# Hybrid decoder trunk on one core: masked copies of the gated heads in two halves a slot apart, the last pair's loads in another order, the fifth block's scores as 384 and 256 columns

## The reference

```python
h = rms_norm(x, norm_g);  proj = h @ w_in                 # split into the groups
# A: 12 heads of 64: dilated windows (128,1), (512,4), (2048,16), mixed by log-sum-exp
# B: 8 heads of 64: causal softmax with bias c[t] - c[s], c = cumsum(log sigmoid(f))
logits = q @ k.T + c[t] - c[s];  p = softmax(causal(logits));  out_b = p @ v
# C: 4 gated linear attention heads, key width 96, value width 192
S_t = diag(alpha_t) S_{t-1} + k_t^T v_t;  out_c = rms_norm(q_t S_t)
mixed = concat([out_a * silu(az), out_b * silu(bz), out_c * silu(cz)])
return x + mixed @ w_out
```

## Time and profile before

| | |
|---|---|
| median of 3 runs | 2104.77 us (2103.35 to 2106.62) |
| profiled execution | 2104.9 us, its span 2103.2 us |
| PE busy | 2050.0 us, 97% |
| DVE busy | 970.3 us, 46% |
| ACT busy | 858.4 us, 41% |
| POOL busy | 249.5 us, 12% |

### The profile page before, as it was taken

How to read it: one execution, slowest core, us unless ns; L and a number is a source line. 1 busy time by engine, 2 the same in 40 slices (tenths; PEclk the granted TensorE clock), 3 DMA queues, 4 the chain that set the end, 5 groups by cost and what they waited for, 6 DMA issues and landing times.

```text
span 2103.2 us, 28249 instructions
## 1 busy us (share of the span) xinstructions
PE 2050.0 (97%) x10120; PEld 1717.1 (82%) x10120; DVE 970.3 (46%) x1579; ACT 858.4 (41%) x1434; POOL 249.5 (12%) x181
## 2 busy tenths in 40 slices
PE   6999999999999999999999999999999988999999
PEld 5778888888878888888888888888888867788887
DVE  6611356455544544554454544554544465512122
ACT  6311344434444444454544444454544454311110
POOL 0000344252420101010010101010010100000000
PEclk9999999999999999999999999999999999999999
DMA  6322323433232222222222222223222363324134
GB/s 224 78 75 65 108 76 104 108 89 108 69 101 76 71 88 58 86 74 89 61 70 85 75 86 86 81 81 100 60 90 85 129 210 113 125 89 130 47 128 150
DMA packets 192457, 201.09 MB, mean 96 GB/s; under 512 B 15993, under 2 KB 141993, under 8 KB 191233
## 3 DMA queue, kind: packets, MB, share of 16 engines
q1 hardware_dynamic: 175664, 169.70, 27.2%
q10 hardware_dynamic: 16720, 30.45, 3.9%
HBM read 151.33 MB, written 48.78 MB: 95 GB/s over the span
## 4 chain that ended last, share of the span: by engine, by line
PE 84%; DVE 7%; ACT 4%; issue 3%; DMA 2%; POOL 1%; SPq 0%; DVEq 0%; ACTq 0%; POOLq 0%
PE acc L1851 18%; PE acc L1853 18%; PE acc L1852 18%; PE pv L2064 4%; PE turned L2049 4%; PE scores L2041 2%; PE scores L2038 2%; DVE w_lo L1360 1%; PE scores L2154 1%; PE scores L2155 1%; PE turned L2155 1%; PE acc L2155 1%; PE scores L2156 1%; PE turned L2156 1%; PE acc L2156 1%
## 5 line engine op out<-in xcount | busy, mean ns | idle before, releaser
L1851 PE MATMUL acc<-act_hi,w_hi 128*128 128x512 f32 x1856 | 743.0, 400 | 7.5 <-DVE act_lo L1391 2.4
L1853 PE MATMUL acc<-act_hi,w_lo 128*128 128x512 f32 x1856 | 725.8, 391 | 0.0
L1852 PE MATMUL acc<-act_lo,w_hi 128*128 128x512 f32 x1856 | 724.2, 390 | 0.0
L1851 PEld LDWEIGHTS acc<-act_hi,w_hi 128*128 128x128 f32 x1856 | 349.4, 188 | 77.1 <-DVE w_lo L1360 5.0
L1853 PEld LDWEIGHTS acc<-act_hi,w_lo 128*128 128x128 f32 x1856 | 348.6, 188 | 76.1
L1852 PEld LDWEIGHTS acc<-act_lo,w_hi 128*128 128x128 f32 x1856 | 349.7, 188 | 65.1
L1360 DVE TENSOR_TENSOR w_lo<-w_raw,w_hi 128x512 fp32r<-128x512 f32 x223 | 196.2, 880 | 317.4 <-ACT w_hi L934 317.4
L1677 DVE TENSOR_TENSOR pt_lo<-turned,pt_hi 128x1024 fp32r<-128x1024 f32 (+1 forms) x120 | 114.9, 958 | 256.0 <-ACT pt_hi L1234 255.0
L1226 ACT ACTIVATE prob<-prob,neg_max 128x128 f32<-128x128 f32 (+7 forms) x160 | 124.1, 776 | 251.5 <-DVE neg_max L1661 251.5
L1234 ACT ACTIVATE pt_hi<-turned 128x1024 fp32r<-128x1024 f32 (+1 forms) x120 | 97.6, 813 | 244.7 <-PE turned L2049 244.7
L934 ACT ACTIVATE w_hi<-w_raw 128x512 fp32r<-128x512 f32 x223 | 139.0, 623 | 128.8 <-PE acc L1853 105.4
(11 more groups left out here) (308 smaller groups left out, 2723.2 us busy)
## 6 DMA issues: line engine op xcount, KB each, us to landing
w_raw<-in_w_in_dram SPq DMA_DIRECT2D x240, 256.0 KB, 2.8
proj_scratch<-stage ACTq DMA_DIRECT2D x116, 256.0 KB, 2.1
w_raw<-in_w_out_dram SPq DMA_DIRECT2D x71, 256.0 KB, 3.0
raw<-proj_scratch SPq DMA_DIRECT2D x20, 512.0 KB, 3.2
act_lo<-mixed_scratch SPq DMA_DIRECT2D x7, 1024.0 KB, 6.7
res<-in_x_dram SPq DMA_DIRECT2D x24, 256.0 KB, 5.5
out_dram<-res SPq DMA_DIRECT2D x24, 256.0 KB, 2.8
extra_raw<-in_w_out_dram SPq DMA_DIRECT2D x23, 256.0 KB, 3.2
```

Source lines behind the costliest of these rows:

```text
L1851: pe.matmul(acc, hi, xh, start=first, stop=False)
L1852: pe.matmul(acc, hi, xl, start=False, stop=False)
L1853: mm = pe.matmul(acc, lo, xh, start=False, stop=end)
```

## The change

Three edits, and nothing else on any engine:

1. `put_first` is cut in two halves. The two copies from `scores` stay in slot 8, the two from `turned` go to slot 9, behind the differences of level 3 and ahead of the copy of level 1.
2. In the last pair SP issues three loads of mixed blocks one by one between rows 4, 5 and 6 instead of all three ahead of row 4; the load of the gate stands behind row 8 instead of row 6, the tiles of x behind row 10 instead of row 7, and the stores of partial sums (with the next tiles of x) behind rows 20 and 35 instead of 18 and 33.
3. Block 4's scores begin at column 128, so that they are 384 and 256 columns.

```diff
 def score_offset(j):
     i = j % NT
-    return HALF * (i % 2) if i < 4 else 0
+    return HALF * (i % 2) if i < 4 else P * (i == 4)
...
-            load_mixed(4)
-            load_mixed(5)
-            load_mixed(6)
             for n in range(4, EARLY):
+                if n < 7:
+                    load_mixed(n)
                 load_early_rows(n)
-                if n == 6:
+                if n == 8:
                     sp.wait_ge(mix_lo, KK_GATED + 1)
                     load_gate(LAST, last_column)
-                if n == 7:
+                if n == 10:
                     sp.wait_ge(silu_done, LAST)
                     for t in range(4):
                         load_early_residual(t)
                 for r, tiles in enumerate(ROUNDS[:-1]):
-                    if n == (KT - 1) * (r + 1) + 3:
+                    if n == (KT - 1) * (r + 1) + 5:
...
-                if slot == G_LEVEL[0] + 2:
-                    put_first(c)
+                for half in range(2):
+                    if slot == G_LEVEL[0] + 2 + half:
+                        put_first(c, half)
...
-            def put_first(c):
-                dve.wait_ge(gla_zero, c + 1)
-                dve.wait_ge(gla_lv, LEVELS * c + 1)
-                for half in range(2):
-                    to = ...
-                    if half > 0:
-                        dve.wait_ge(gla_put, levels_put)
-                    put(to, ident_both..., pieces[half][:, :, :, 0:P])
+            def put_first(c, half):
+                if half == 0:
+                    dve.wait_ge(gla_zero, c + 1)
+                    dve.wait_ge(gla_lv, LEVELS * c + 1)
+                to = ...
+                if half > 0:
                     dve.wait_ge(gla_put, levels_put)
-                    put(to..., level_mask[:, 0, :, :]..., pieces[half][:, :, :, P:])
+                put(to, ident_both..., pieces[half][:, :, :, 0:P])
+                dve.wait_ge(gla_put, levels_put)
+                put(to..., level_mask[:, 0, :, :]..., pieces[half][:, :, :, P:])
...
-                pe.wait_ge(masked, ITEMS * pair + j - (o > 0))
+                pe.wait_ge(masked, ITEMS * pair + j - (o == HALF))
                 q = q_st[:, h, i * P:(i + 1) * P]
-                for c0 in range(0, n, HALF):
-                    c1 = min(c0 + HALF, n)
+                edge = min(HALF - o % HALF, n)
+                for c0, c1 in ((0, edge), (edge, n))[:1 + (edge < n)]:
```

More of the change, by code:

```diff
@@ L1568, in put @@
                 dve.copy_predicated(dst, mask.bitcast(I32), data).then_inc(gla_put, 1)
-            def put_first(c):
-                dve.wait_ge(gla_zero, c + 1)
-                dve.wait_ge(gla_lv, LEVELS * c + 1)
-                for half in range(2):
-                    to = weights_t[:, half * HALF:(half + 1) * HALF].rearrange("p (b u q) -> p b u q", b=2, u=2)
-                    if half > 0:
-                        dve.wait_ge(gla_put, levels_put)
-                    put(to, ident_both[:, :, :].unsqueeze(1).broadcast_to([P, 2, 2, P]), pieces[half][:, :, :, 0:P])
+            def put_first(c, half):
+                if half == 0:
+                    dve.wait_ge(gla_zero, c + 1)
+                    dve.wait_ge(gla_lv, LEVELS * c + 1)
+                to = weights_t[:, half * HALF:(half + 1) * HALF].rearrange("p (b u q) -> p b u q", b=2, u=2)
+                if half > 0:
                     dve.wait_ge(gla_put, levels_put)
-                    put(to.rearrange("p b u (n two) -> p b u n two", two=2)[:, :, :, :, 1],
-                        level_mask[:, 0, :, :].unsqueeze(1).broadcast_to([P, 2, 2, HEAD]),
-                        pieces[half][:, :, :, P:])
+                put(to, ident_both[:, :, :].unsqueeze(1).broadcast_to([P, 2, 2, P]), pieces[half][:, :, :, 0:P])
+                dve.wait_ge(gla_put, levels_put)
+                put(to.rearrange("p b u (n two) -> p b u n two", two=2)[:, :, :, :, 1],
+                    level_mask[:, 0, :, :].unsqueeze(1).broadcast_to([P, 2, 2, HEAD]), pieces[half][:, :, :, P:])
             def put_level(c, l):
```

## The result

| | before | changed |
|---|---|---|
| median | 2104.56 us (2101.37 to 2106.62, 6 runs) | 2116.53 us (2112.18 to 2118.62, 6 runs) |
| profiled execution, its span | 2104.9, 2103.2 | 2112.18, 2110.4 |
| PE's mean granted clock, profiled | 0.993 | 0.991 |

The profiled execution of the changed kernel is the fastest of its six; the others took 2116.0 to 2118.6.

What follows compares the result with a forecast made beforehand. PE, busy almost throughout, was taken as the bound, so only its work or idle time counts. Terms of -1.8, -6.7 and +3.2 sum to -5.3 from 2104.77: 2099.5 us, stated range 2093.5 to 2105.5.

Steps and rivals of the forecast that it cites:

- Edit 3: Block 4's scores: 0.09 us less PE time in each of 20 items, -1.8 us, bounds -1.0 and -2.0.
- Edit 2: Last pair: quarter 7 starts 3.6 us earlier and quarter 11 6.7 earlier; -6.7 us, bounds -6.2 and -9.2.
- Rival B: Last pair: the next wait takes the gain, quarter 11 hardly earlier; -1 instead of -6.7, 2105.2 us; chance 0.15.
- Edit 1, levels 3 and 4: Gated heads: the level 3 wait goes, PE waits about 1.5 us at level 4, which starts 0.8 later.
- Rival A: Gated heads: differences come 1.7 us earlier and both waits go; -0.65 a head, -2.6, 2093.7 us; chance 0.20.
- Level 5 is 0.3 us in time again, level 6 more. So each head loses 0.8: Gated heads after level 4: no further delay at later levels, so +3.2 us in four heads.
- Rival C: Gated heads: the new 1.5 us wait at level 4 drops the clock, 1.7 to 2.5 us more where it falls; chance 0.15.

Runs made afterwards that it cites:

- last_pair_gate_row6: The kernel before with only the last pair's load order changed, but the gate's load kept behind row 6: 2101.51 us, ratio 0.999.
- halves_back_early: The kernel before with the two `turned` copies a slot later and ACT's reversed copy of the values two slots earlier: 2108.47 us, ratio 1.0022.
- halves_only: The kernel before with only the two copies from `turned` moved a slot later: 2125.12 us, ratio 1.0097.

## Why the prediction was wrong

Two of its three terms came out as forecast; the third, edit 1, had the right delay and missed one of its consequences.

**Edit 3: right in the records.** -1.8 was said, -1.9 is there for ten pairs; the medians cannot confirm it.

**Edit 2: right.** Quarter 7 lost its wait, quarter 11 came 6.7 earlier and still waits 3.27 (3.4 was said), and the edit alone gives 6.7 to 7.0 at the median. DVE's score step of block 6 began at 1736.52, 1722.69 without the offset of 13.83, where 1722.66 was said. Its cause was given a little too narrowly: last_pair_gate_row6 keeps some 2 us without moving the gate's load. Rival B falls.

**Edit 1, levels 3 and 4: right.** Second head, with the offset of 3.89: the second difference of level 4 was to end at 356.5 + 3.89 = 360.4, and the exponential behind it began at 360.42; `q_tile` was to end at 361.3 + 3.89 = 365.2, and PE's level 4 began at 365.24. The wait is 1.5, and level 4 is 365.24 - 360.62 - 3.89 = 0.73 later. Rival A falls: the second difference of level 3 ended at 353.65 + 1.76 - 3.89 = 351.52, which is 0.27 earlier than before and not 1.7. DVE, second head, a difference of level 1, the first copy from `scores`, both differences of level 3, a copy from `turned`; then POOL's instruction beside the first of these copies:

```profile
345.76 0.68 DVE L1518 TENSOR_TENSOR g_t<-g_b 96x512 f32<-96x512 f32 x1
...
350.31 0.75 DVE L1568 COPY_PREDICATED logit_bias<-ident_both,scores 128x512 f32<-128x512 int32 x1 [2.07 <-PE turned L1931]
...
352.51 1.21 DVE L1518 TENSOR_TENSOR g_t<-g_b 96x512 f32<-96x512 f32 x1
353.65 1.76 DVE L1519 TENSOR_TENSOR g_t<-g_b 96x512 f32<-96x512 f32 x1
355.33 0.73 DVE L1568 COPY_PREDICATED logit_bias<-ident_both,turned 128x512 f32<-128x512 int32 x1
...
349.81 1.54 POOL L882 TENSOR_TENSOR q_tile<-g_qd,g_t 96x512 f32<-96x512 f32 x1
```

The differences of level 3 take 1.21 and 1.76 beside POOL's work, where that of level 1, without POOL beside it, took 0.68. The copy with its data in PSUM takes 0.75 beside POOL's `q_tile`, and 0.73 at 355.33, where POOL is idle. The Trainium skill ("SBUF — State Buffer", section "Who interferes with whom") has the rule that a DVE instruction with two SBUF inputs contends with GpSimd's reads and one with a single SBUF input does not. The trace agrees.

**The step that failed** is "Level 5 is 0.3 us in time again, level 6 more. So each head loses 0.8". It followed POOL's `q_tile`, the one releaser that the earlier trace rows name, and passed over what stands between levels 4 and 5 on PE: the transposes of the values, whose releaser is ACT. Level 5 itself was in time, as said: its `q_tile` ended at 368.71 + 1.27 = 369.98, and PE came to it at 371.97, or at 370.5 without the new wait. But the exponential of level 5 was late with DVE's differences, and the values' copy behind it had 0.24 us in hand. This wait of 1.4 brings the loss from 0.8 to 2.4 a head, 9.5 us in four instead of 3.2. halves_back_early shows that: with the copy elsewhere the loss is 0.8 a head and 4.8 us in all.

**The clock** took the rest, 6 us in the profiled execution of the changed kernel and 4 x 3.3 = 13 in that of halves_only. The prediction gave it nothing in the gated heads, and named a granted clock below 1.00 there as a sign that it was wrong. Rival C had the mechanism but not its condition. It asked whether a wait of 1.5 is long enough, and held 0.15 for it; a wait of 1.5 alone kept 1.00 in three heads, and one of 1.25 alone in four. Waits of 1.5 and 1.4 (1.9 and 1.3 in the first head) with 369.62 - 1.44 - 367.04 = 1.1 us of work between them dropped the clock in all heads of halves_only, and in three of four in the changed kernel. C's highest time, 2109.5, was too low as well, since it had the waits at 0.8 a head. What made the second head of the changed kernel the exception is open.

## What to carry to other kernels

When a step on one engine comes later, list everything that stands behind it in that engine's program, and every engine that waits for any of it, not only the releaser that the view of waits names: a wait that is hidden by 0.24 us has no row there. An instruction that depends on nothing late should not stand behind one that does; here the place of such a copy of 1.04 us decided over some 17 us. And cost waits by their neighbourhood: two waits that were each harmless to the clock of PE cost 3.3 us a head in clock, beside 2.4 in waiting, when they came one behind the other.

## What the runs showed of the hardware

- Single waits of PE of 1.25 and 1.5 us, in busy surroundings, left the granted clock at 1.00; one of 1.92 took it to 0.89 over 16 us. Two of 1.5 and 1.4 close together (1.9 and 1.3 in the first head) took it to 0.79 over 16 us in all four heads of halves_only, and to 0.89, 1.00, 0.89 and 0.79 in those of the changed kernel.
- DVE's difference of 96 x 512 with both inputs in SBUF took 0.68 us alone and 1.21 and 1.76 beside POOL's products; its copy from PSUM took 0.73 alone and 0.75 beside them.
- A row of 256 KB behind the 512 KB of the gate was used by ACT 5.71 us after its issue with four tiles of x behind it, and 4.35 after with three rows ahead of these. The tiles and rows behind it are 256 KB each; why it landed sooner is not shown.
